# Modulation vectors moved from the pool stage into the differential attention, and the pool counts cut to 16 rows

## The reference, cut to what matters

```python
count = jnp.arange(1, S + 1)                       # pool mixer, window w
mean = (cs - lag) / jnp.minimum(count, float(w))[None, :, None]
feats.append(mean - ug)
...
c_act = jax.nn.silu(c)                             # second block, layer l
shift, scale, gate = jnp.split(c_act @ ada_w[l] + ada_b[l], 3, axis=-1)
h = rms_norm(x, norm_w[l]) * (1.0 + scale[:, None, :]) + shift[:, None, :]
```

## Time and profile before

| | us |
|---|---|
| median of 3 runs | 4192.17 (4188.13 to 4193.98) |
| the profiled execution's own time | 4184.91 |
| its span, first to last instruction | 4183.1 |
| busy over the span: PE, DVE, ACT, POOL | 3535.2, 2417.4, 1808.9, 283.5 |
| mean granted clock of TensorE, 1 being 2.4 GHz | 0.916 |
| differential attention, first score to last output | 300.3 to 559.4 |
| pool stage, from its first load to its last store's issue | 1438.9 to 1652.9 |

### The profile page before, as it was taken

One profiled execution on the slowest core, in us unless ns is written; L12 is line 12 of the kernel. 1 busy time (PEld: TensorE's weight loads), 2 busy tenths in 40 slices (PEclk: granted clock), 3 DMA queues, 4 the chain that ended last, 5 costly groups with the idle time before them and its releaser, 6 DMA issues. The chain is left out here.

```text
span 4183.1 us, 52718 instructions
## 1 busy us (share of the span) xinstructions
PE 3535.2 (85%) x17556; PEld 2685.6 (64%) x17556; DVE 2417.4 (58%) x3882; ACT 1808.9 (43%) x2971; POOL 283.5 (7%) x358
## 2 busy tenths in 40 slices
PE   8989977799999186959999936998968789998687
PEld 7866656688887043748888825786744477777343
DVE  3326665899987556569998965512335454033455
ACT  2216641688886100138888823314433232144232
POOL 0000010000000200000000020000011100000111
PEclk9989988899999598969999967999979989999798
DMA  6222242799998745539999964412133244221321
GB/s 236 99 71 65 58 140 103 283 399 398 398 399 308 256 163 191 183 116 399 399 398 399 398 233 173 169 64 57 44 114 105 68 163 158 69 52 34 137 85 59
DMA packets 404379, 799.19 MB, mean 191 GB/s; under 512 B 99174, under 2 KB 149894, under 8 KB 400008
## 3 DMA queue, kind: packets, MB, share of 16 engines
q1 hardware_dynamic: 381196, 713.40, 47.3%
q0 software_dynamic: 13824, 50.34, 3.4%
q10 hardware_dynamic: 9216, 33.56, 2.0%
HBM read 661.25 MB, written 135.95 MB: 191 GB/s over the span
## 5 line engine op out<-in xcount | busy, mean ns | idle before, releaser
L314 DVE TENSOR_TENSOR experts_down_lo<-weights_down,experts_down_hi 128x1024 fp32r<-128x1024 f32 x256 | 301.5, 1221 | 54.7 <-ACT experts_down_hi L310 52.4
L314 DVE TENSOR_TENSOR experts_gate_lo<-weights_gate,experts_gate_hi 128x1024 fp32r<-128x1024 f32 x256 | 299.0, 1221 | 55.1 <-ACT experts_gate_hi L310 50.4
L310 ACT CAST experts_gate_hi<-weights_gate 128x1024 fp32r<-128x1024 f32 x256 | 254.4, 1055 | 110.7 <-PEq L128 67.8
L314 DVE TENSOR_TENSOR experts_up_lo<-weights_up,experts_up_hi 128x1024 fp32r<-128x1024 f32 x256 | 296.2, 1219 | 1.2 <-ACT experts_up_hi L310 0.5
L363 PE MATMUL project_acc<-project_wh,project_hh 128*128 128x512 f32 (+2 forms) x768 | 285.6, 372 | 0.0
L364 PE MATMUL project_acc<-project_wl,project_hh 128*128 128x512 f32 (+2 forms) x768 | 281.9, 367 | 0.0
L365 PE MATMUL project_acc<-project_wh,project_hl 128*128 128x512 f32 (+2 forms) x768 | 281.8, 367 | 0.0
L310 ACT CAST experts_down_hi<-weights_down 128x1024 fp32r<-128x1024 f32 x256 | 256.6, 1052 | 28.0 <-DMA weights_down<-in_moe_w_down_dram 27.8
L2551 PE MATMUL mixout_acc<-mixout_w,mixout_mT 128*128 128x512 f32 x512 | 255.0, 651 | 13.7 <-ACT mixout_mT L2633 10.5
L310 ACT CAST experts_up_hi<-weights_up 128x1024 fp32r<-128x1024 f32 x256 | 254.8, 1057 | 8.3 <-DMA weights_up<-in_moe_w_up_dram 6.8
L363 PE MATMUL experts_yp<-experts_down_hi,experts_hTh 128*128 128x512 f32 x512 | 209.9, 410 | 13.1 <-DVE experts_hTl L314 13.1
(11 more groups left out here) (425 smaller groups left out, 7893.6 us busy)
## 6 DMA issues: line engine op xcount, KB each, us to landing
weights_gate<-in_moe_w_gate_dram SPq DMA_DIRECT2D x256, 512.0 KB, 13.4
weights_up<-in_moe_w_up_dram SPq DMA_DIRECT2D x256, 512.0 KB
weights_down<-in_moe_w_down_dram SPq DMA_DIRECT2D x256, 512.0 KB
scratch_y<-experts_y ACTq DMA_DIRECT2D x64, 512.0 KB, 6.3
pool_ada<-in_ada_w_dram SPq DMA_DIRECT2D x16, 1536.0 KB, 7.4
mixout_row<-scratch_proj SPq DMA_DIRECT2D x16, 1368.0 KB, 5.9
project_raw<-in_w_in_dram SPq DMA_DIRECT2D x8, 2048.0 KB
scratch_proj<-project_row SPq DMA_DIRECT2D x64, 256.0 KB, 2.0
```

The costliest lines, as they stand in the source:

```text
L310: return act.copy(hi, src)
L314: return dve.tensor_tensor(lo, src, hi.bitcast(F32), ALU.subtract)
```

## The change

1. The modulation is worked out in the differential attention. SP loads `c`, both biases and both rows of `norm_w` as columns (5 transfers, in which each element of the tensor in DRAM is 4 bytes at a stride) and then 6 slabs of `ada_w`, all ahead of the loop over heads; the other 10 slabs follow, 3 in each head, each after a wait for `added`.
2. A slab is scaled by ACT (`scale`, one instruction over 128 x 3072) and added by POOL (`add`, a `tensor_tensor` over 128 x 3072, none for a layer's first slab, which ACT writes straight into the accumulator). ACT's 16 instructions stand at the end of steps 0, 1, 3, 4, 6, 7, and so on to 22, behind the four exponentials. ACT's `silu` stands ahead of the loop.
3. `total` becomes 24 matmuls with a single column of ones, for each layer, in steps 14 and 28 of PE, into spare columns of the output's PSUM bank; ACT copies them out (`take`), POOL adds the bias, adds 1 to the scale and multiplies by `norm_w` (`finish`), and SP stores three columns of vectors back as rows, element by element, in heads 5 and 7.
4. From the pool stage all of the modulation goes: 16 additions and 12 copies of DVE, 12 matmuls of 512 columns of PE, POOL's fills, the slabs' transfers.
5. The inverse counts are loaded for the first 16 rows alone (4 x 16 floats, 4 transfers), and the window's product with them covers 16 columns. For the other 1008 columns one `scalar_tensor_tensor` multiplies by 1/window and subtracts `u`; one short subtraction does the first 16.

```diff
+    STAGES = 6
+    MK = 3 * D // P
+    AHEAD = 3
+    TOTAL_AT = (14, 28)
+    FIRST_AFTER = 12
...
+        self.w = ph.sb("ada", [P, self.STAGES, 3 * D])
+        self.acc = ph.sb("ada_sum", [P, 2, 3 * D])
+        self.ones = ph.sb("ones", [P, 1])
...
     def load_small(self, nc, sp):
+        with nc.allow_non_contiguous_dma(reason="vectors as columns"):
+            sp.dma_start(self.cs[:, :], self.c.rearrange("o (k p) -> p (o k)", p=P)).then_inc(self.small_in, 16)
+            for l in range(2):
+                sp.dma_start(self.bias[:, l, :], self.ada_b[l:l + 1, :].rearrange("o (k p) -> p (o k)", p=P)).then_inc(self.small_in, 16)
+                sp.dma_start(self.nw[:, l, :], self.norm_w[l:l + 1, :].rearrange("o (k p) -> p (o k)", p=P)).then_inc(self.small_in, 16)
...
     def load(self, sp, n):
+        if n >= self.STAGES:
+            sp.wait_ge(self.added, n - self.STAGES + 1)
...
     def silu(self, act):
-        act.wait_ge(self.c_in, 16)
+        act.wait_ge(self.small_in, 16 * 5)
...
+    def scale(self, act, n):
+        l, k = divmod(n, KC)
+        u = n % self.STAGES
+        w = self.w[:, u, :]
...
+        act.wait_ge(self.w_in[u], 16 * (n // self.STAGES) + 16)
+        act.activation(self.acc[:, l, :] if k == 0 else w, w, ACT.Copy, scale=self.cs[:, k:k + 1]).then_inc(self.scaled, 1)
...
+    def add(self, pool, n):
+        pool.wait_ge(self.scaled, n + 1)
...
+        if k == 0:
+            pool.sem_inc(self.added, 1)
+        else:
+            pool.tensor_tensor(acc, acc, self.w[:, n % self.STAGES, :], ALU.add).then_inc(self.added, 1)
...
+    def total(self, nc, pe, l, bank):
+        pe.wait_ge(self.ones_set, 1)
         pe.wait_ge(self.added, KC * l + KC)
+        for k in range(self.MK):
+            last = nc.tensor.matmul(bank[:, k:k + 1], self.acc[:, l, k * P:(k + 1) * P], self.ones[:, :], start=True, stop=True)
+        last.then_inc(self.m_ready, 1)
...
+    def store(self, nc, sp, l):
+        sp.wait_ge(self.m_done, l + 1)
+            for r, part in enumerate((1, 0, 2)):
+                sp.dma_start(self.mods[l, r:r + 1, :].rearrange("o (k p) -> p (o k)", p=P),
+                             self.cols[:, l, part * KC:(part + 1) * KC]).then_inc(self.m_stored, 16)
...
@@ phase_attention, sync
                 load_q(1)
                 load_v(1)
+                if m:
+                    m.load_small(nc, sp)
+                    for n in range(m.STAGES):
+                        m.load(sp, n)
...
+                    if m:
+                        for n in range(m.STAGES + m.AHEAD * h, min(m.STAGES + m.AHEAD * (h + 1), 2 * KC)):
+                            m.load(sp, n)
+                        if h == 5:
+                            m.store(nc, sp, 0)
+                        if h == HEADS - 1:
+                            m.store(nc, sp, 1)
+                            sp.wait_ge(m.m_stored, 16 * 6)
...
@@ phase_attention, tensor: in step n, after the wait for o_done
+                    if m and n in m.TOTAL_AT:
+                        m.total(nc, pe, m.TOTAL_AT.index(n), o_ps[:, 0, dv:])
...
@@ phase_attention, scalar
+                if m:
+                    m.silu(act)
                 for n in range(N):
...
                         for mp in range(maps):
                             exp(n + 1, 1, mp)
+                    if m and n % 3 < 2 and n // 3 * 2 + n % 3 < 2 * KC:
+                        m.scale(act, n // 3 * 2 + n % 3)
...
@@ phase_pool
-                sp.dma_start(inv_count[:, :, :], counts.partition_broadcast(P)).then_inc(small_in, 16)
+                for g in range(NG):
+                    sp.dma_start(inv_count[:, g, :], counts[:, g * SEQ:g * SEQ + PADW].partition_broadcast(P)).then_inc(small_in, 16)
...
-                    if g == NG - 1:
-                        m.total(nc, pe, 1)
                     outputs(g)
-                    if g == 1:
-                        m.total(nc, pe, 0)
...
-                    ch(dve.tensor_tensor(s[:, n % 2, PADW:], src[:, PADW:], inv_count[:, g, :], ALU.mult))
-                    ch.wait()
+                    ch(dve.tensor_tensor(edge[:, :], src[:, PADW:2 * PADW], inv_count[:, g, :], ALU.mult))
...
-                    dve.tensor_tensor(pT[:, ct % CG, :], s[:, n % 2, PADW:], u[:, PADW:], ALU.subtract).then_inc(p_ready, 1)
+                    ch(dve.scalar_tensor_tensor(pT[:, ct % CG, PADW:], src[:, 2 * PADW:], 1.0 / POOL_WINDOWS[g], u[:, 2 * PADW:],
+                                                ALU.mult, ALU.subtract))
+                    ch.wait()
+                    dve.tensor_tensor(pT[:, ct % CG, 0:PADW], edge[:, :], u[:, PADW:2 * PADW], ALU.subtract).then_inc(p_ready, 1)
...
                 for ct in range(CG):
                     window(ct)
-                    adds(ct)
```

More of the change, by code:

```diff
@@ L229, in __init__ @@
         self.cs = ph.sb("c", [P, KC])
-        self.w = ph.sb("ada", [P, 2, 3 * D])
-        self.acc = ph.sb("ada_sum", [P, 3 * D])
-        self.nw = ph.sb("nw", [1, D])
-        self.rows = ph.sb("mod_rows", [1, 3, D])
-        self.ones = ph.sb("ones", [P, P])
-        self.bank = ph.ps("mod", [P, 2, HALF])
-        self.w_in = [ph.sem(f"ada_in{u}") for u in range(2)]
-        self.c_in, self.b_in, self.nw_in, self.cleared, self.c_act, self.added, self.m_ready, self.m_done, self.m_stored = (
-            ph.sem(n) for n in ("c_in", "b_in", "nw_in", "cleared", "c_act", "ada_added", "mod_ready", "mod_done", "mod_stored"))
@@ new lines, in __init__ @@
+        self.acc = ph.sb("ada_sum", [P, 2, 3 * D])
+        self.ones = ph.sb("ones", [P, 1])
+        self.bias, self.nw = ph.sb("ada_bias", [P, 2, self.MK]), ph.sb("nw", [P, 2, KC])
+        self.cols = ph.sb("mod_cols", [P, 2, self.MK])
+        self.w_in = [ph.sem(f"ada_in{u}") for u in range(self.STAGES)]
+        self.small_in, self.ones_set, self.c_act, self.scaled, self.added, self.m_ready, self.m_taken, self.m_done, self.m_stored, self.own = (
+            ph.sem(n) for n in ("ada_small", "ones_set", "c_act", "ada_scaled", "ada_added", "mod_ready", "mod_taken", "mod_done", "mod_stored", "mod_own"))
@@ new lines, in take, with finish @@
+    def take(self, act, l, bank):
+        act.wait_ge(self.m_ready, l + 1)
+        act.copy(self.cols[:, l, :], bank[:, 0:self.MK]).then_inc(self.m_taken, 1)
+    def finish(self, pool, l):
+        ch = Chain(pool, self.own, 2 * l)
+        cols = self.cols[:, l, :]
+        pool.wait_ge(self.m_taken, l + 1)
+        ch(pool.tensor_tensor(cols, cols, self.bias[:, l, :], ALU.add))
+        ch.wait()
+        scale = cols[:, KC:2 * KC]
+        ch(pool.tensor_scalar(scale, scale, 1.0, None, ALU.add))
+        ch.wait()
+        pool.tensor_tensor(scale, scale, self.nw[:, l, :], ALU.mult).then_inc(self.m_done, 1)
@@ L309, in part_hi @@
+    def store(self, nc, sp, l):
+        sp.wait_ge(self.m_done, l + 1)
+        with nc.allow_non_contiguous_dma(reason="columns back to rows"):
+            for r, part in enumerate((1, 0, 2)):
+                sp.dma_start(self.mods[l, r:r + 1, :].rearrange("o (k p) -> p (o k)", p=P),
+                             self.cols[:, l, part * KC:(part + 1) * KC]).then_inc(self.m_stored, 16)
 def part_hi(act, hi, src):
@@ L592, in _, with phase_attention @@
                     angles.reduce(dve)
-def phase_attention(nc, K, name, q, k, v, out, maps, dk, dv, mask, scale, totals, lam_parts=None):
+def phase_attention(nc, K, name, q, k, v, out, maps, dk, dv, mask, scale, totals, lam_parts=None, modulation=None):
     PAIRS = TILES // 2
@@ L853, in _ @@
                             exp(n + 1, 1, mp)
+                    if m and n % 3 < 2 and n // 3 * 2 + n % 3 < 2 * KC:
+                        m.scale(act, n // 3 * 2 + n % 3)
                 if diff:
                     evacuate(N - 1)
+            @block.gpsimd
+            def _(pool):
+                if m:
+                    pool.memset(m.ones[:, :], 1.0).then_inc(m.ones_set, 1)
+                    for n in range(2 * KC):
+                        if n == m.FIRST_AFTER:
+                            m.finish(pool, 0)
+                        m.add(pool, n)
+                    m.finish(pool, 1)
             @block.vector
```

112 lines of the change are left out of this document (22 added, 90 removed).

## The result

The changed kernel takes 4227.05 us, median of 5 runs (4216.16 to 4234.66); the kernel before took 4192.17 (4186.45 to 4193.98, 5 runs) beside it. The ratio is 1.0082, 95% interval 1.0060 to 1.0103: slower, 34.9 us by the medians. The profiled executions differ by 45.3 us of span (4228.4 against 4183.1).

What follows compares the result with a forecast made beforehand. PE was taken as nearly the bound in the attention; in the pool stage it waited for DVE. Terms -31.5 + 17 + 10 + 1.5 = -3.0 gave a 4189 us median; 8-in-10 range 4171 to 4213.

Steps and rivals of the forecast that it cites:

- Pool stage: Pool stage: modulation gone, shorter windows on DVE, PE starting about 5.0 us earlier; gain 26.5 + 5.0 = 31.5 us.
- The last group: Pool stage's end: PE waits 7.4 us for tile 7's window, then restarts slowly, 2.7 us added.
- Scalings, `silu`, start: Attention on ACT: 16 scalings delay PE's awaited copy by 0.62 us on average, 9.8 alone; start 1.5 for function tables.
- The rival of dear elements: Attention start: loads at 3 us per 1024 elements hold `silu` until about 330; +15 us, 4207; chance 0.10.
- Length of an addition and the lock: Attention: a POOL addition takes 6.6 us and holds DVE's two-input instruction until done, blocking 2.8 or 3.1 us.
- What the lock costs: Attention: most of DVE's blocked time falls into slack; without the lock the forecast would be 7 us lower.
- Blocked 3.1 ... left 1.0. Average 0.8: Attention, one step on: DVE's `combine` blocked 3.1 us, slack 2.1, 1.0 left; average of both steps 0.8.
- I give them no price of their own: Attention: maxima behind `combine` on DVE and ACT's next exponentials start late with it; no separate price.
- Totals: Attention on PE: 24 fp32 matmuls per layer, two instructions each at 0.12 us; 5.0 us each, 10 for both.
- The far bound, 21: Attention on PE: upper bound for the totals at 0.22 us each, what a matmul of 256 columns takes; 21 us.
- The end: Attention's end: stores by elements issued in head 7 cost nothing, or up to 5 us if dear.
- The rival of the lock-out: Attention, at `combine`: DVE locked out by slower additions, decisive from 7.5 us each; at 8.7, +26, 4218; chance 0.13.

Runs made afterwards that it cites:

- run 5: Changed kernel without POOL's additions and without the two totals; 4165.37 us, against 4192.48 for the kernel before.
- run 4: Kernel before with only the 16 inverse counts and the one-instruction window end, modulation left in the pool stage; 4181.67 us, ratio 0.9979.
- runs 6: Changed kernel with scalings and whole additions in every second step, totals at steps 16 and 31; 4229.76 us.
- run 8: Changed kernel with the odd-numbered additions (second of each pair, and two alone) cut into twelve pieces; 4194.70 us.
- run 1: Changed kernel with POOL's 14 additions left out, scalings and totals kept; 4187.26 us, ratio 0.9997 to the kernel before.
- run 12: Changed kernel without additions, each total's 24 matmuls spread over four steps, six at a time; 4180.19 us.
- run 3: Changed kernel with each POOL addition replaced by a POOL fill of the same 3072 columns; 4186.02 us.
- run 9: Changed kernel with the even-numbered additions (first of each pair) cut into twelve pieces, the odd ones whole; 4203.60 us.
- run 11: Changed kernel with additions in pieces, totals in the first mixture layer's combine, vectors transposed and stored as 512-byte rows; 4171.59 us, ratio 0.9949.
- run 10: Changed kernel with additions in pieces, totals in the first mixture layer's combine, vectors stored element by element between row tiles; 4184.36 us, ratio 0.9988.

## Why the prediction was wrong

Of the profiled execution's span the forecast made -3.0 us and the trace +45.3. Term by term:

- **Pool stage: right in sum.** -31.5 forecast, -31.2 measured, of two parts that missed the opposite way: PE started 3.2 us earlier, not 5.0 (32.6 after the first load for 35.8; the kernels with the new counts range from 31.1 to 32.6), and its row took 28.0 less, not 26.5. That they made up for each other is luck. The last group came as forecast: a wait of 7.32 (7.4), and outputs 2.1 slower (2.7).
- **Scalings, `silu`, start: too dear.** 9.8 + 1.5 = 11.3 forecast; 6.2 measured for 15 of the 16 scalings, 0.41 each instead of 0.62, and 0.1 for the start with the first scaling (28.2 in run 5, 28.1 in run 4). A scaling took 2.86 (2.9). The five transfers by elements landed by 312.6 (forecast: about 312). The rival of dear elements is out for the loads.
- **Length of an addition and the lock: right.** 6.69 (6.6); seven ratios lasted 3.3 to 3.5, two 2.7 (2.8 and 3.1 of waiting forecast).
- **What the lock costs: the step that failed.** "Blocked 3.1 ... left 1.0. Average 0.8", 7 us for all additions; measured 43.6 between the marks (45.1 by the whole attention). For a first addition 0.8 was nearly right (1.1 in runs 6 and 8). The second of a pair I had meet only the ratio of its own combine, as if VectorE were on time. I did not carry the first delay on to the instructions behind it on VectorE and hold their times against the next addition's start: they lie 8.1 and 8.3 us behind the first addition's start (359.59 and 359.73 against 351.46), and a few tenths decide over 6.3 us: a join that began 0.52 ahead of the addition was free, one that began 0.05 ahead was not. Nor did I price the maxima behind the join ("I give them no price of their own"), and through them everything waits: no slack takes up 6.3 us. This is 36 of the 48.3 us of error.
- **Totals: mis-sized.** Twice 5.0 forecast; twice 8.8 by runs 1 and 5. Step by step the first cost 8.0 in run 1; the second cost 8.1 in the changed kernel (its step took 15.0 us for 6.9) and 9.7 in run 1 (16.6). The pace that I took from the earlier trace rows, 0.12, was right at the full clock (0.117 in run 12). What I left out is that the clock falls in a row of one-column matmuls, so that the rest of the total and the outputs behind it run at half pace. The far bound, 21, held. 6 to 8 us.
- **The end: 3.5 us, forecast as nothing.** The last head's store was issued at 632.21, though its output was copied by 630.95; before, it followed at once (559.41 and 559.44). By the kernel's text SP stands there until the stores by elements have landed. In run 3 it stood 2.2 us so. That is inside the bound of 5 us that I gave; the other 2.3 are open.
- **The rest:** 2.9 ahead of step 2, where run 4 is as late without the modulation, and 4.3 in stretches that the change doesn't touch, where kernels without the additions differ by as much. So about 7 us of the 45.3 are not the change's by anything shown here. The medians differ less than the spans (34.9), since the profiled execution of before lay under its median.

The rival of the lock-out had the right place and direction, but the wrong switch: it asked for additions above 7.5 us. At 6.7 two additions in a row did it.

## What to carry to other kernels

Where two engines lock each other, a long instruction's price is not its overlap in a single step: shift every later instruction of the held engine by the delay, and look which of them now meets the next long one. Cut such work into short instructions; that costs the unpressed engine 45% more time here, and the pressed one nearly nothing. Before work is moved to an engine's idle time, its small ends count too: two rows of 48 one-column instructions on the bounding engine cost 16 to 18 us, and 6144 single-element stores 14 us; the one wanted a stage in which PE idles, the other a transpose. And before a small price is read from one execution of each kernel, compare the stage in a kernel that leaves it alone: here the starts alone differed by 3 us, more than 14 additions in pieces cost.

## What the runs showed of the hardware

- A VectorE instruction with two inputs from SBUF that met a running GpSimd addition of 6.7 us lasted until its end, to within 0.3 us: over one column up to 4.54 us instead of 0.22 (run 9), over 128 or 256 columns 6.80 to 6.86 instead of 0.35 or 0.48 (changed). One that began 0.52 us ahead of the addition was not held, one that began 0.05 ahead was. VectorE's maxima, read from PSUM, kept their length beside an addition (2.35 us for two of 1024 columns, at 426.45, as before). Fills met no such instruction, so nothing is shown of them.
- TensorE's granted clock fell to 0.50 while it was busy without a gap with one-column fp32 matmuls (run 1, from 436). They come at 0.117 us each at the full clock (1.40 / 12, run 12) and at 0.217 at 0.50 (10.40 / 48, run 11). In run 8 it also fell in a row of scores, with no total near.
- Elements of 4 bytes were cheap to load on quiet queues (9216 by 312.6, issued from 301). Their stores took longer: the last 3072 of the changed kernel, issued from 613.28 to 614.89, held SP until 632.21, some 17 us, with the DMA share at 0.06 and less from 616 on. Beside row loads they cost most: the next rows came about 5 us late each in run 10 (11.8 to 12.8 us of waiting, 6.5 and 7.1 in run 11).
